# A 24-part transformer forward pass on one core: state-space chunks and linear attention written out, and another order at the opening of the streams

## What is computed

```python
def gla_chunked(k, v, log_a, q, s0, with_output):        # chunks of 64, 4 heads, K 64, V 128
    b = jnp.cumsum(log_a, axis=2); b_last = b[:, :, -1]
    d_state = einsum('bnlhk,bnlhv->bnhkv', k * exp(b_last[:, :, None] - b), v)
    # s_(n+1) = exp(b_last) * s_n + d_state
    q_dec = q * exp(b)
    o_inter = einsum('bnlhk,bnhkv->bnlhv', q_dec, s_prev)
    scores = where(tri, einsum('bnlhk,bnshk->bnhls', q_dec, k * exp(-b)), 0.0)
    return o_inter + einsum('bnhls,bnshv->bnlhv', scores, v)

def ssd_chunked(x, bm, dt, cm, s0, with_output, a_coef): # chunks of 128, 4 groups, 8 heads of 64
    acum = jnp.cumsum(dt * a_coef, axis=2); a_last = acum[:, :, -1]; xdt = x * dt[..., None]
    states = einsum('bclgn,bclgh,bclghp->bcghpn', bm, exp(a_last[:, :, None] - acum), xdt)
    # s_(n+1) = exp(a_last) * s_n + states
    y_off = einsum('bclgn,bcghpn->bclghp', cm, s_prev) * exp(acum)[..., None]
    decay = exp(where(tri, seg, -inf)); cb = einsum('bclgn,bcsgn->bcgls', cm, bm)
    return y_off + einsum('bcgls,bcghls,bcsghp->bclghp', cb, decay, xdt)
# after it: y + d_skip * x
```

## Time and profile before

| | us |
|---|---|
| median of 3 runs | 5276.81 (5272.70 to 5281.71) |
| the profiled execution | 5279.67 |
| its span | 5277.9 |

### The profile page before, as it was taken

One profiled execution on the slowest core, in us unless ns is written; L12 is line 12 of the kernel. 1 busy time (PEld: TensorE's weight loads), 2 busy tenths in 40 slices (PEclk: granted clock), 3 DMA queues, 4 the chain that ended last, 5 costly groups with the idle time before them and its releaser, 6 DMA issues. The chain is left out here.

```text
span 5277.9 us, 86568 instructions
## 1 busy us (share of the span) xinstructions
PE 4397.3 (83%) x35688; PEld 3709.9 (70%) x35688; DVE 2395.0 (45%) x3418; ACT 1495.6 (28%) x2486; POOL 582.8 (11%) x795
## 2 busy tenths in 40 slices
PE   7687799999895688759979586499999985757998
PEld 5555688888753588749967475388888883436997
DVE  4445343345356444454434323343336835664444
ACT  2254321122243212122213312221223324442221
POOL 2011100001013322110001000000001113310000
PEclk8898899999996799979989755799999997768999
DMA  4437222223377422133323222222222334443332
GB/s 160 140 115 232 78 64 64 60 60 95 127 235 263 140 50 48 38 97 95 93 68 98 86 67 74 99 59 64 65 60 75 109 112 142 142 142 85 93 94 73
DMA packets 687000, 536.15 MB, mean 102 GB/s; under 512 B 128877, under 2 KB 613489, under 8 KB 686672
## 3 DMA queue, kind: packets, MB, share of 16 engines
q1 hardware_dynamic: 657424, 440.76, 27.9%
q0 software_dynamic: 29248, 90.63, 4.8%
HBM read 447.18 MB, written 84.11 MB: 101 GB/s over the span
## 5 line engine op out<-in xcount | busy, mean ns | idle before, releaser
L87 PE MATMUL acc<-h_hi,w_hi 128*128 128x258 f32 (+2 forms) x4416 | 1402.1, 317 | 46.0 <-DVE h_lo L456 39.4
L89 PE MATMUL acc<-h_hi,w_lo 128*128 128x258 f32 (+2 forms) x4416 | 1398.2, 317 | 0.0
L88 PE MATMUL acc<-h_lo,w_hi 128*128 128x258 f32 (+2 forms) x4416 | 1396.8, 316 | 0.0
L87 PEld LDWEIGHTS acc<-h_hi,w_hi 128*128 128x128 f32 x4416 | 832.5, 189 | 113.8 <-DVE h_lo L456 23.5
L88 PEld LDWEIGHTS acc<-h_lo,w_hi 128*128 128x128 f32 x4416 | 833.4, 189 | 60.4 <-issue 0.5
L89 PEld LDWEIGHTS acc<-h_hi,w_lo 128*128 128x128 f32 x4416 | 833.0, 189 | 59.0
L335 ACT CAST w_hi<-staged 128x1024 fp32r<-128x1024 f32 (+1 forms) x414 | 406.9, 1028 | 540.9 <-PE acc L89 390.0
L443 DVE TENSOR_TENSOR w_lo<-staged,w_hi 128x1024 fp32r<-128x1024 f32 (+1 forms) x414 | 480.4, 1200 | 138.8 <-ACT w_hi L335 135.9
L87 PE MATMUL acc<-hidden_hi,w_hi 128*128 128x512 f32 (+1 forms) x1200 | 420.0, 350 | 67.5 <-DVE hidden_lo L574 67.5
L484 DVE COPY offset<-acc 128x2 f32<-128x2 f32 x276 | 43.8, 159 | 929.1 <-PE acc L89 926.3
L88 PE MATMUL acc<-hidden_lo,w_hi 128*128 128x512 f32 (+1 forms) x1200 | 419.5, 350 | 0.0
(11 more groups left out here) (457 smaller groups left out, 6683.6 us busy)
## 6 DMA issues: line engine op xcount, KB each, us to landing
staged<-in_w_ffn_in SPq DMA_DIRECT2D x88, 512.0 KB, 4.5
staged<-in_ffn_w_in SPq DMA_DIRECT2D x88, 512.0 KB, 4.6
wmod<-in_w_mod SPq DMA_DIRECT2D x8, 3072.0 KB, 10.9
wmod<-in_mod_w SPq DMA_DIRECT2D x8, 3072.0 KB, 13.2
wmod<-in_mod_w SPq DMA_DIRECT2D x16, 1536.0 KB, 9.3
rows<-acum SPq DMA_DIRECT2D x48, 512.0 KB, 4.0
staged<-in_ssd_w_in SPq DMA_DIRECT2D x42, 512.0 KB, 4.7
wmod<-in_w_mod SPq DMA_DIRECT2D x8, 2048.0 KB, 8.2
```

Of the source, the lines that this page charges most:

```text
L87: nc.tensor.matmul(out, w[0], x[0], start=start, stop=False)
L88: nc.tensor.matmul(out, w[0], x[1], start=False, stop=False)
L89: return nc.tensor.matmul(out, w[1], x[0], start=False, stop=stop)
```

## The change

**Streams.** With a source, SP waits until the last rows have landed before it loads the second half of the first weight tile; ACT and DVE do the first half, the rows, then the second half. With the norm first, `prepare` starts at once, and the two halves are done behind its second and fourth call.

**Linear attention.** All twelve chunks are written out. The state lies above the turned values in one tile of 128 rows (`state_v`), the queries above the masked scores (`q_scores`), so that one product does what two did. To land on the lower partitions the keys are turned by a product with the identity, and the values are padded with 64 zero columns ahead of their 64 tokens (eight memsets on POOL, which SP's first loads wait for). There are four slots of loads. The first load comes before masks and decays; the front of chunk i+1 is ahead of the core of chunk i.

**State-space chunks.** All four groups are written out, with fixed addresses. `xf`, `bf`, `xt`, `bt` are double, `cf` is there for each group, `rows` and `last` four times, `y` four times. The fills of the next group stand one behind each item on PE (`fill(g + 1, w)`), and their copies on ACT two items later. The weighing of item w+1 is ahead of the state of item w. The state update is eight `scalar_tensor_tensor`, one for each head, in place of `faded` and the sum; the first items copy from PSUM, and the two memsets go. Context items need no rows for `w < 2`. SP stores `y` four items back, in its own list. `ssd_scan` is called before the tile `wide` is allocated.

```diff
                         if not (p.g0 == 0 and is_step(i, 0)):
                             sp.wait_ge(S["w_ready"], 2 * i + (2 * p.g0 + j - 1))
+                        elif j and source is not None:
+                            sp.wait_ge(S["x_loaded6"], 16)
...
-                split_hi(phases[0], 0, 0)
+                norm_first = phases[0].stats == 0
+                if not norm_first:
+                    split_hi(phases[0], 0, 0, (0,) if source is not None else (0, 1))
                 if source is not None:
                     for k in range(0, KD, 2):
...
+                    split_hi(phases[0], 0, 0, (1,))
                 act.wait_ge(S["factor_ready"], 1)
-                if phases[0].stats == 0:
+                if norm_first:
                     shift_columns(0)
                     for kt in range(KD):
                         prepare(None, kt // 2, kt % 2, 0)
+                        if kt in (1, 3):
+                            split_hi(phases[0], 0, 0, (kt // 2,))
...
@@ gla_chunks @@
+                load(0)
+                sp.dma_start(masks[:], masks_src).then_inc(S["masks_loaded"], 16)
...
+                for i in range(1, NCH):
+                    load(i)
...
-                            nc.tensor.matmul(b_ps[d][:, 0, h], kqr[s][d][:, 0, h], kqr[s][d][:, 1, h], start=True, stop=True)
+                            nc.tensor.matmul(b_ps[d][low, 0, h], keys[s][d][:, 0, h], q_scores[s][d][top, h], start=True, stop=True)
...
-                            mm = nc.tensor.transpose(b_ps[d][:, 1, h], kqr[s][d][:, 2, h], ident[0:GK, 0:GK])
+                            mm = nc.tensor.matmul(b_ps[d][low, 1, h], keys[s][d][:, 1, h], ident[top, top], start=True, stop=True)
...
-                            nc.tensor.matmul(o_ps[d][:, h], state[d][:, h], kqr[s][d][:, 1, h], start=True, stop=False)
-                            mm = nc.tensor.matmul(o_ps[d][:, h], vt[d][:, h], sc[d][:, h], start=False, stop=True)
+                            mm = nc.tensor.matmul(o_ps[d][:, h], state_v[s][d][:, h], q_scores[s][d][:, h], start=True, stop=True)
...
+                front(0)
+                for i in range(NCH):
+                    if i + 1 < NCH:
+                        front(i + 1)
+                    core(i)
...
@@ ssd_groups @@
+                        if g == 0 and w == 4:
+                            load(1)
+                        if w == 7 and g + 2 < SG:
+                            load(g + 2)
+                        store(g * NW + w - 4)
...
+                    if f >= 2:
+                        pe.wait_ge(S["emptied"], g * KEPT + (f - 1))
+                    elif g and f == 1:
+                        pe.wait_ge(S["emptied"], g * KEPT)
+                    elif g:
+                        pe.wait_ge(S["cb_c"], 2 * g)
...
+                        if g + 1 < SG and w < FILLS:
+                            fill(g + 1, w)
...
+                        if g + 1 < SG and 2 <= w < KEPT + 2:
+                            keep(g + 1, w - 2)
...
+                    for h in range(SH):
+                        op = V.scalar_tensor_tensor(out=state[d][:, h], in0=state[d][:, h], scalar=last[f % 4][:, h:h + 1],
+                                                    in1=grow_ps[d][:, h], op0=ALU.mult, op1=ALU.add)
...
+                for g in range(SG):
+                    masked(g)
+                    weigh(g, FIRST)
+                    for w in range(FIRST):
+                        grow(g, w)
+                    for w in range(FIRST, NW):
...
+                        if w + 1 < NW:
+                            weigh(g, w + 1)
+                        grow(g, w)
...
-                    V.tensor_tensor(faded[d][:], state[d][:], spread(last[d][:], HD), ALU.mult).then_inc(S["faded_c"], 1)
...
-                    V.tensor_tensor(state[d][:], faded[d][:], grow_ps[d][:], ALU.add).then_inc(S["state_c"], 1)
...
-                    pool.dma_start(ys[d][(c - SCC) * SC:(c - SCC + 1) * SC, bass.ds(g * GW, GW)],
-                                   y[d][:].rearrange("p h v -> p (h v)")).then_inc(stored[d], 16)
```

More of the change, by code:

```diff
@@ L2350, in gla_chunks @@
         two = lambda n, shape: [sb(f"{n}{d}", shape) for d in range(2)]
-        sc = two("sc", [CH, GH, CH])
-        kr = two("kr", [CH, GH, GK])
-        vt = two("vt", [CH, GH, GV])
-        state, scaled = two("state", [GK, GH, GV]), two("scaled", [GK, GH, GV])
-        o = [[sb(f"o{s}{d}", [GV, GH, CH]) for d in range(2)] for s in range(2)]
+        kr, o = pair("kr", [P, GH, GK]), pair("o", [GV, GH, CH])
+        scaled = two("scaled", [GK, GH, GV])
+        top, low = slice(0, GK), slice(GK, P)
@@ new lines, in gla_chunks, with order, columns @@
+        names = ["dec_loaded", "masks_loaded"] + [f"loaded{s}" for s in range(SLOTS)] + [
+            "padded", "cleared", "sc_p", "v_p", "sc_c", "kr_c", "vt_c", "grown_p", "o_p", "scaled_c", "state_c", "o_c", "stored0", "stored1"]
+        with stage(nc, *names) as (block, *sems):
+            S = dict(zip(names, sems))
+            loaded, stored = [S[f"loaded{s}"] for s in range(SLOTS)], (S["stored0"], S["stored1"])
+            def order(i, d):
+                return i if d == 0 else (NCH + CC - 1 if i >= CC else CC - 1) - i
+            def columns(i, d):
+                return slice(order(i, d) * CH, order(i, d) * CH + CH)
@@ L2452, in _ @@
+                rows(0)
+                for i in range(NCH):
+                    if i + 1 < NCH:
+                        rows(i + 1)
+                    for d in range(2):
+                        act.wait_ge(S["o_p"], 2 * i + (d + 1))
+                        if i >= 2:
+                            act.wait_ge(stored[i % 2], 32 * (i // 2))
+                        nc.scalar.copy(o[i % 2][d][:], o_ps[d][:]).then_inc(S["o_c"], 1)
             @block.vector
             def _(dve):
-                for d in range(2):
-                    nc.vector.memset(state[d][:], 0.0).then_inc(cleared, 1)
@@ L2480, in _, with scores @@
-                both_phases(dve, step)
+                def scores(i):
+                    s = i % SLOTS
+                    for d in range(2):
+                        dve.wait_ge(S["sc_p"], 2 * i + (d + 1))
+                        m = masks[low, d, 1, :].rearrange("p (o c) -> p o c", o=1).to_broadcast([CH, GH, CH])
+                        nc.vector.tensor_tensor(q_scores[s][d][low], b_ps[d][low, 0], m, ALU.mult).then_inc(S["sc_c"], 1)
+                for d in range(2):
+                    nc.vector.memset(state_v[0][d][top], 0.0).then_inc(S["cleared"], 1)
@@ L2482, in _ @@
             @block.gpsimd
             def _(pool):
[L2484 to L2485 removed]
+                for s in range(SLOTS):
                     for d in range(2):
[L2487 to L2489 removed]
+                        nc.gpsimd.memset(vf[s][d][:, :, 0:CH], 0.0).then_inc(S["padded"], 1)
```

559 lines of the change are left out of this document (262 added, 297 removed).

## The result

| | median us | runs |
|---|---|---|
| before | 5277.15 | 4 (5272.70 to 5281.71) |
| changed | 5139.10 | 4 (5133.91 to 5139.64) |

The ratio is 0.9736, with a 95% interval of 0.9719 to 0.9753: 138 us less, where 131 were forecast (5146, range 5108 to 5182). The profiled execution of the changed kernel lasts 5139.12 with a span of 5137.2, against 5279.67 and 5277.9.

A forecast was written before the change was run, and what follows sets the result against it. PE's instruction list was taken to bound linear attention, and no single engine the state-space chunks. Linear attention -32, state-space -76 and openings -23 sum to -131 us: 5148.7 for a profiled execution, 5146 as median, range 5108 to 5182.

The forecast's parts named there:

- the hand-over: Linear attention: front moved ahead of core may win 0.1 to 0.4 us at each of four a chunk, or nothing.
- Rival C: Linear attention: the clock rises with merged products of 128 rows; -60 us, 5086; chance 0.10.
- collisions: State-space chunks: POOL's products stretch DVE's two-SBUF operations by 0.84 for nearly each of 8 items; 6 us a group.
- the head: State-space groups: DVE stands 6.5 us before the first weighing, behind ACT's ordered copies; 9 us put on groups 2 and 3.
- rival F: State-space chunks: ACT waits for decay rows each item, because SP, blocked at a store's wait, issues late; +160, 5306; 0.02.
- the four slots: State-space chunks: SP's waits for y precede row loads, but four slots and the 4.0 us landing cover them.
- the last group: State-space chunks: no turnings to insert, so 1 us for the head, less 3 for missing turnings; 44 us long.
- the wait for load 1: First state-space group: load 1 is issued behind five transfers, so its weighing is some 7 us late; group 69 us.
- Behind a mixer: Three openings: rows go before the second weight tile, so PE starts earlier; 6.5 us each for two, 5 for the smaller.
- With the norm first: Two openings: ACT starts squares at once, but splits now lie between them; 2.5 us each (0 to 4).
- Rivals B and E: State-space chunks: B, POOL holds the port, 28 us more, 5174, 0.18; E, turnings do not hide, +20, 5166, 0.02.
- the two large terms: Linear attention -32 us (ends -22 and -45) and state-space chunks -76 us (ends -110 and -48).

The follow-up runs named there:

- the pair of runs above: Linear attention with growth products taken in turn with next chunk's scores and turnings, 5069.97 us; and the same order with all in one quarter, 5138.69 us.

## Why the prediction was right

**Linear attention.** The chain "PE is the bound, its list shrinks, the clock stays" held: the clock is 0.50, the merged products cost 1.73 and 1.90 against 1.8 priced from the earlier trace rows, the turnings +0.43. Mis-sized was the hand-over, which the text left at nothing, or down to -12 more: it gave 12 to 13 (a chunk of 12.19 for 13.3). Most of its mechanism wasn't in the text. The change puts growth products on the lower rows and scores into the lower half, so that they share the array: the two growth groups of a chunk took 3.65 us before (3080.70 to 3082.59 and 3086.19 to 3087.95) and take 2.80 now (1.89 and 0.91), 10 us in all. The scores of a chunk take 1.81 for 2.03, another 2 to 3 us in all, the value turnings as long as before (1.96 for 1.98); only these scores can be the hand-overs that the text had in mind. The opening came 0.8 earlier, where 1 to 4 later was estimated.

**Rival C**, the rise of the clock, had the wrong trigger. Merged products with 128 rows did not raise it; in the order in which small products overlap it rose. Overlap and clock together took 73 to 77 us from the stage, where the text priced the clock alone at 60. The Trainium skill (TensorE: Matmul & The Clock Gate, Part 3) says that small products placed in different parts of the array run at the same time in it; the pair of runs above agrees, 3.61 against 1.90 us. Its Part 1, sustained activity releases the throttle, is not enough here: PE was busy for 120.00 of 120 us at 0.50.

**State-space chunks.** The price of the update was right (1.61 for 1.6). Groups 1 and 2 were 54.3 and 54.4 in the windows for 54. Inside that, two terms offset each other: collisions are 4, not 6, and the head is longer than the 9 put on it (8.2 of idle, then 3.4 in three waits behind the first weighing). For the head the text named only ScalarE's order; 1.8 of the 8.2 us were the rows behind SP's store, rival F's mechanism in a small form, which the text had dismissed by the four slots. The worst term is the last group: 44 forecast (its own terms, 39 and 6 and 1 less 3, give 43), 54.2 measured. It was given 1 us for its head and credited with the missing turnings, but VectorE stood for 9.45, since without turnings ScalarE waits for the rows: with stores one item later it was 2.1 shorter, with the context updates in front 6.9. The first group was 4.4 longer than its 69, in which the wait for load 1 was named; what made up the difference wasn't tested. Together the groups took 236.3 us for 222, 14 too many. The row missed by only 8.5, because 5.9 were won in the two places beside the groups that no term named. That part is luck, and so is that linear attention erred by 12 the other way.

**Openings.** Behind a mixer 5.1, 5.9 and 6.0 for 6.5, 5 (the one with 512 tokens) and 6.5, by the mechanism named: the order on ScalarE and VectorE. What SP's wait adds to it couldn't be told. With the norm first the streams gained 3.5 and 4.4 for 2.5 each, and that they gained as much is luck: from SP's first load PE starts 0.55 and 0.75 us earlier, not 2.5, because the first low part takes 2.83 for 1.23 beside POOL. The gain comes mostly behind the first product. In the first stream VectorE has its last low part at 68.4 for 70.9, and PE's waits before its next pieces are 1.27, 2.54 and 2.18 for 2.48, 2.55, 2.53 and 0.99.

**Rivals B and E** were wrong in what they feared: no weighing lasted over 2.06, and the distance from last y to next weighing is 10.05, 10.48 and 11.33 us, inside the 8 to 20 given. That the total came within 7 us is in good part luck, since the two large terms missed by 12 and 8.5 to opposite sides; the mechanisms named for each of them were there.

## What to carry to other kernels

When PE is busy all the time and still granted 0.50, ask which quarters of the array its products use before asking what hides them: two products of 64 rows in different quarters cost hardly more than one (eight growth instructions took 1.89 us alone and 1.90 together with the 16 of scores and turnings), and here the clock rose to 1.00 with that order. At the head of a loop whose engines are all nearly busy, follow each engine's own list, SP's included: a store that waits for the last result in front of the next loads makes them late, by about 2 us at each of three places here. And work that is needed by nobody else until later belongs inside a wait, not behind it.

## What was not expected of the hardware

- Products of 64 rows run beside each other if their rows or their results lie in different halves, and follow each other if both are equal: 1.90 (both different) against 3.61 us (both equal) for the same 24 instructions at 1.2 GHz. With only one of the two different, the last three growth products of a chunk still started in turn with the scores.
- The granted clock followed the work and not the busy time: 0.50 with PE busy for 120.00 of 120 us, 1.00 with the same instructions in different quarters, though only from some 15 us after the start of the stage, and it fell again for ten us behind a wait of 1.51 us for loads. What exactly decides was not settled. Warm turnings in front of the stage held it for a few us only.
- A state update of eight small operations with one operand in PSUM (1.61 us) beats two large ones (1.23 and 0.69) by 15 us over 32 items, although it is more instructions: POOL doesn't stretch it. Some 4 of the 15 us are the weighings, which last longer with the two.
